# Diagonal and neighbour scores of a recurrence: a sum over partitions by a matrix of ones, in F32R

## The reference, cut to what matters

```python
q = silu(xn @ w_q)
forget = lb + (1 - lb) * sigmoid(xn @ w_f)
log_f, k, v = log(forget), 1 - forget, xn @ w_i
# for each head (8 heads, 128 channels d) and each chunk of time:
b = cumsum(log_f)                                    # over the times of the chunk
o_inter = (q * exp(b)) @ state
scores[t, s] = sum_d q[t, d] * k[s, d] * exp(b[t, d] - b[s, d])   # s <= t, else 0
o = o_inter + scores @ v
state = exp(b_last) * state + (k * exp(b_last - b)).T @ v
```

## Time and profile before

| | us |
|---|---|
| median of 3 runs | 2204.59 (2203.95 to 2204.7) |
| profiled execution, its own time | 2202.08 |
| its span in the profile | 2200.3 |
| PE busy | 2175.3 (99%) |
| DVE busy | 1475.7 (67%) |
| ACT busy | 987.3 (45%) |
| POOL busy | 936.6 (43%) |
| mean granted clock of TensorE | 0.999 |

### The profile page before, as it was taken

One profiled execution on the slowest core, in us unless ns is written; L12 is line 12 of the kernel. 1 busy time (PEld: TensorE's weight loads), 2 busy tenths in 40 slices (PEclk: granted clock), 3 DMA queues, 4 the chain that ended last, 5 costly groups with the idle time before them and its releaser, 6 DMA issues.

```text
span 2200.3 us, 29937 instructions
## 1 busy us (share of the span) xinstructions
PE 2175.3 (99%) x11390; PEld 1828.2 (83%) x11390; DVE 1475.7 (67%) x1967; ACT 987.3 (45%) x1338; POOL 936.6 (43%) x256
## 2 busy tenths in 40 slices
PE   8999999999999999999999999999999999999998
PEld 6888887787798897888887798897788887898887
DVE  6999998777656468877867666467666515656333
ACT  5353564524343344666555343344566524243333
POOL 3444444544553553423224453554411244453542
PEclk9999999999999999999999999999999999999999
DMA  5233332422223333222122223332322222233322
GB/s 199 96 106 106 106 124 74 156 89 86 96 96 102 110 99 103 58 77 58 56 66 88 96 96 96 100 111 80 101 53 62 72 82 91 96 97 101 119 77 77
DMA packets 230851, 206.65 MB, mean 94 GB/s; under 512 B 13905, under 2 KB 220369, under 8 KB 230481
## 3 DMA queue, kind: packets, MB, share of 16 engines
q1 hardware_dynamic: 227328, 199.36, 29.0%
q10 hardware_dynamic: 3408, 5.70, 0.7%
HBM read 194.02 MB, written 4.19 MB: 90 GB/s over the span
## 4 chain that ended last, share of the span: by engine, by line
PE 88%; issue 5%; DVE 3%; POOL 2%; ACT 1%; DMA 0%; POOLq 0%; SPq 0%; ACTq 0%; DVEq 0%
PE ps L2035 15%; PE ps L2037 15%; PE ps L2036 15%; PE ps L2068 5%; PE ps L2069 5%; PE ps L2070 5%; PE ps L2268 5%; PE ps L2266 5%; PE ps L2267 5%; PE ps L2400 2%; POOL w_lo L643 2%; PE ps L2607 2%; PE ps L2568 2%; PE ps L2596 1%; DVE ps L1584 1%
## 5 line engine op out<-in xcount | busy, mean ns | idle before, releaser
L643 POOL TENSOR_TENSOR w_lo<-raw,w_hi 128x2048 fp32r<-128x2048 f32 x149 | 712.9, 4784 | 992.6 <-ACT w_hi L694 982.2
L694 ACT ACTIVATE w_hi<-raw 128x2048 fp32r<-128x2048 f32 x148 | 283.4, 1915 | 523.7 <-PE ps L2037 370.2
L2035 PE MATMUL ps<-XH,w_hi 128*128 128x512 f32 x576 | 228.9, 397 | 0.0
L2037 PE MATMUL ps<-XH,w_lo 128*128 128x512 f32 x576 | 227.5, 395 | 0.0
L2036 PE MATMUL ps<-XL,w_hi 128*128 128x512 f32 x576 | 227.5, 395 | 0.0
L2035 PE MATMUL ps<-FH,w_hi 128*128 128x512 f32 x528 | 208.7, 395 | 0.0
L2036 PE MATMUL ps<-FL,w_hi 128*128 128x512 f32 x528 | 208.6, 395 | 0.0
L2037 PE MATMUL ps<-FH,w_lo 128*128 128x512 f32 x528 | 208.6, 395 | 0.0
L1597 DVE TENSOR_TENSOR ps<-ps,rst 128x1024 f32<-128x1024 f32 (+1 forms) x52 | 55.5, 1067 | 185.7 <-PE ps L2037 136.4
L656 POOL TENSOR_TENSOR w_lo<-raw,w_hi 128x1024 fp32r<-128x1024 f32 x35 | 96.9, 2768 | 175.7 <-ACT w_hi L882 175.7
L1338 DVE SCALAR_TENSOR_TENSOR ps<-UP,vec,ps 128x512 f32<-128x512 f32 x224 | 148.6, 744 | 0.0
(11 more groups left out here) (434 smaller groups left out, 5657.1 us busy)
## 6 DMA issues: line engine op xcount, KB each, us to landing
raw<-in_w SPq DMA_DIRECT2D x64, 512.0 KB, 4.3
raw<-in_mlp_w_up SPq DMA_DIRECT2D x64, 512.0 KB, 4.4
raw<-in_mlp_w_down SPq DMA_DIRECT2D x64, 512.0 KB, 4.3
raw<-in_w_in SPq DMA_DIRECT2D x56, 512.0 KB, 4.6
raw<-in_mla_w_o SPq DMA_DIRECT2D x16, 512.0 KB, 5.0
raw<-in_w_b_out SPq DMA_DIRECT2D x16, 384.0 KB, 3.8
raw<-in_w_a_out SPq DMA_DIRECT2D x8, 512.0 KB, 4.5
raw<-in_w_o SPq DMA_DIRECT2D x8, 512.0 KB, 3.9
```

The costliest lines, as they stand in the source:

```text
L643: pool.tensor_tensor(w_lo[:, s], raw[:, s], w_hi[:, s].bitcast(F32), ALU.subtract)\
L694: act.activation(w_hi[:, s], raw[:, s], ACT.Copy).then_inc(hi_done, 1)
L2035: pe.matmul(dst, his[k], xh[k], start=start and k == 0, stop=False)
L2037: mm = pe.matmul(dst, los[k], xh[k], start=False, stop=stop and k == n - 1)
```

## The change

The diagonal score and the neighbour score no longer come from block products. DVE makes the products over all channels elementwise, HD = HQ * HK (512 columns) and HN = exp * k * q (256 columns, one for each pair). ACT rounds them to F32R (HDH, HNH), DVE makes the rest (HDL, HNL). PE multiplies with ONES, a 128x128 matrix of ones, in two passes (high and low), which puts the sum over the channels into every partition; the masks keep the same places as before. HDL and HNL lie at the addresses of HD and HN. The last level's subtraction, exponential and products run on half as many elements for the decay: one subtraction in place of two, 256 columns of Exp in place of 512, two products of 256 as before, the second waiting for the first. The semaphores used are ones that an earlier stage has left. Where the new steps stand in each engine's order is in the diff:

```diff
@@ ACT
+            act.activation(ONES[:], ones[:], ACT.Copy).then_inc(ff_sem("h_one"), 1)
             act.wait_ge(s_("f_gain"), 2)
...
@@ def decays_act
                 for l in range(len(LEVELS)):
                     act.wait_ge(s_("h_arg"), 14 * h + 2 * l + 2)
-                    act.activation(HE[:, l], HE[:, l], ACT.Exp).then_inc(s_("h_e"), 1)
+                    e = HE[:, l] if l < len(LEVELS) - 1 else HE[:, l].rearrange("p (g u) -> p g u", u=2)[:, :, 1]
+                    act.activation(e, e, ACT.Exp).then_inc(s_("h_e"), 1)
+                act.wait_ge(*ff("h_d", h + 1))
+                act.activation(HDH[:], HD[:], ACT.Copy).then_inc(ff_sem("h_dh"), 1)
+
+            def next_act(h):
+
+                act.wait_ge(s_("h_qk"), 14 * h + 14)
+                act.activation(HNH[:], HN[:], ACT.Copy).then_inc(ff_sem("h_nh"), 1)
@@ def head_act
                     gates_act(h + 1, split=(lambda: split_hi(2 * h + c + 4, 0)) if first else None)
+                if first:
+                    next_act(h)
                 out_gate_act(h, n)
...
                 square_out(h)
+                if more:
+                    next_act(h + 1)
@@ def decays_dve
+                    if m == 1:
+                        dve.tensor_tensor(ev[:, :, 1], bv[:, :, 1], bv[:, :, 0], ALU.subtract).then_inc(s_("h_arg"), 2)
+                        continue
@@ def decayed_dve
+                    if m == 1:
+                        next_ = HN[:].rearrange("p (g t) -> p g t", t=1)
+                        dve.tensor_tensor(next_, ev[:, :, 1], kv[:, :, 0], ALU.mult).then_inc(ff_sem("h_n"), 1)
+                        dve.wait_ge(*ff("h_n", h + 1))
+                        dve.tensor_tensor(next_, next_, qv[:, :, 1], ALU.mult).then_inc(s_("h_qk"), 2)
+                        continue
@@ DVE
+            def same_dve(h):
+
+                dve.wait_ge(s_("hq_done"), h + 1)
+                dve.wait_ge(s_("hk_done"), h + 1)
+                dve.tensor_tensor(HD[:], HQ[:], HK[:], ALU.mult).then_inc(ff_sem("h_d"), 1)
+
+            def same_low_dve(h):
+
+                dve.wait_ge(*ff("h_dh", h + 1))
+                dve.tensor_tensor(HDL[:], HD[:], HDH[:].bitcast(F32), ALU.subtract).then_inc(ff_sem("h_dl"), 1)
+
+            def next_low_dve(h):
+
+                dve.wait_ge(*ff("h_nh", h + 1))
+                dve.tensor_tensor(HNL[:], HN[:], HNH[:].bitcast(F32), ALU.subtract).then_inc(ff_sem("h_nl"), 1)
@@ def head_dve
                 if more and not first:
                     gates_dve(h + 1)
+                if not first:
+                    next_low_dve(h)
                 levels_dve(h, range(2 if first else 0, 4))
                 if more:
                     floor_dve(h + 1)
                 else:
                     keep_dve(0)
+                if first:
+                    next_low_dve(h)
                 levels_dve(h, (4,))
...
                 levels_dve(h, (7,))
                 if more:
+                    same_dve(h + 1)
                     decays_dve(h + 1, range(3, len(LEVELS)))
                     keys_to_end_dve(h + 1, 1 - n)
                     rest_dve(h + 1, 1 - n)
                     decayed_dve(h + 1, 1 - n)
+                    same_low_dve(h + 1)
@@ DVE, head 0
             decays_dve(0, range(len(LEVELS)))
+            same_dve(0)
             keys_to_end_dve(0, 0)
             decayed_dve(0, 0, range(2), last=False)
+            same_low_dve(0)
             rest_dve(0, 0)
@@ def diagonal
                 pe.wait_ge(s_("h_t1"), h + 1)
-                pe.wait_ge(s_("hq_done"), h + 1)
-                for b in range(TB):
-                    t = slice(b * P, (b + 1) * P)
-                    mm = pe.matmul(ps[:, 6, t], HK[:, t], HQ[:, t], start=True, stop=True)
-                mm.then_inc(s_("h_g"), 1)
+                pe.wait_ge(*ff("h_one", 1))
+                pe.wait_ge(*ff("h_dl", h + 1))
+                pe.matmul(ps[:, 6], ONES[:], HDH[:], start=True, stop=False)
+                pe.matmul(ps[:, 6], ONES[:], HDL[:], start=False, stop=True).then_inc(s_("h_g"), 1)
@@ def level
                 pe.wait_ge(s_("h_qk"), 14 * h + 2 * l + 2)
+                if m == 1:
+                    pe.wait_ge(*ff("h_nl", h + 1))
+                    pe.matmul(ps[:, 4 + l % 2, 0:HALF], ONES[:], HNH[:], start=True, stop=False)
+                    pe.matmul(ps[:, 4 + l % 2, 0:HALF], ONES[:], HNL[:], start=False, stop=True)\
+                        .then_inc(s_("h_g"), 1)
+                    return
```

More of the change, by code:

```diff
@@ L189, in build_program @@
             ("FR", [P, T], F32),
+            ("HD", [P, T], F32), ("HDH", [P, T], F32R), ("HN", [P, HALF], F32), ("HNH", [P, HALF], F32R),
+            ("ONES", [P, P], F32R),
         ]
@@ L195, in build_program @@
             at_h += size + (-size) % 32
-        HR, HZ, HQ, HK, HF, HGATE, HVF, HV, HE, HP, HQD, HKD, HEB, reset, HKT, HS, masks, FR = made
+        HR, HZ, HQ, HK, HF, HGATE, HVF, HV, HE, HP, HQD, HKD, HEB, reset, HKT, HS, masks, FR, HD, HDH, HN, HNH, ONES = made
+        HDL, _ = place("HDL", [P, T], F32R, at_h - (4 * T + 4 * T + 4 * HALF + 4 * HALF + 4 * P))
+        HNL, _ = place("HNL", [P, HALF], F32R, at_h - (4 * HALF + 4 * HALF + 4 * P))
         AH, _ = place("AH", [P, HEADS_M, T], F32R, a_xh)
@@ L268, in build_program @@
             "part_kept": ("lru_done", 15), "u_y": ("mu_add", 7), "u_f": ("xc_done", 8), "u_fh": ("uh_done", 8),
-            "u_fl": ("yb_evac", 8), "root_2": ("ch_done", 2), "d_scaled": ("v_part", 36),
+            "u_fl": ("yb_evac", 8), "root_2": ("ch_done", 2), "h_d": ("lam_abs", 2), "h_dh": ("ln_inv", 2), "h_dl": ("pads", 2),
+            "h_n": ("mu_mm", 1), "h_nh": ("var_mm", 1), "h_nl": ("r_row", 1), "h_one": ("lam_e", 1), "d_scaled": ("v_part", 36),
         }
```

## The result

| | before | after |
|---|---|---|
| median, us | 2204.27 (2200.58 to 2204.7, 4 runs) | 2258.14 (2256.74 to 2259.41, 4 runs) |
| profiled execution, its own time | 2202.08 | 2256.74 |
| its span | 2200.3 | 2254.9 |
| mean granted clock | 0.999 | 0.988 |
| PE busy, share of the span | 2175.3 (99%) | 2187.8 (97%) |

The ratio is 1.0248, 95% interval 1.023 to 1.0266: slower by 2.5%. The forecast was 2239 us with a range up to 2254. The sign, the place and the first links of the chain were right. Which instructions stand still, and what the lower clock costs, came out otherwise.

A forecast was written before the change was run, and what follows sets the result against it. PE, busy 99%, was taken to bound the kernel, its gains eaten by new waits. Profiled 2202.08 + 30.2 for waits + 4 for the clock + 2.5 from profiled execution to median = 2239 us, range 2213 to 2254.

The forecast's parts named there:

- E: Mark in each head: the end of DVE's last decayed product, from which the prediction counts its + times.
- The failed step: DVE behind OL: POOL's second instruction takes the lock after X, HNL stands until +14.4, level 2 at about +15.7.
- rival 1: POOL's second instruction starts later or HNL slips in: 0.68 us per head, +10.1 in all, 2215 us; chance 0.15.
- rival 2: POOL takes the lock twice in a row ahead of OL: 1.25 us more per head, 2246 us; chance 0.09.
- The mis-sized term: PE's lower clock after idling in six heads: 4 us taken, bounds 0 and 10.
- L: Mark in each head: PE starts the block of level 2, 11.67 us after E before the change.
- heads 1 to 6, E to L: Late POOL splits and DVE's standing HNL delay level 2: 4.03 us per head, six times, 24.2.
- heads 1 to 6, L to E, clock in it: Behind the last level's copy DVE has 0.37 us more per head; the lower clock adds 4.
- head 0, up to E of head 1: DVE's prologue grows 0.87 us and next_low_dve adds 0.34, +1.2; DVE's later work before E adds 0.37.
- head 7, E to L: No second split, but PE waits for the late chunk: L at E + 12.06 against 9.19, +2.9 us.
- The upper bound: Clock loss between L and the last copy in every one of six heads: 6 x 1.7 = 10 us, sum +40.
- rival 3: PE stays the bound and its 8.0 us come off, 2197 us; chance 0.08 with its partial form.

The follow-up runs named there:

- the wait alone: Kernel before, with only a wait on ACT at the end of each head for the next head's last decayed product: 2252.56 us, ratio 1.0231.
- the filler: Changed kernel with 30 unused F32R matmuls of 256 columns on PE ahead of level 2 in heads 1 to 6: 2243.8 us, ratio 1.0193.
- ACT's move alone: Changed kernel with ACT's HNH copy moved behind the root and the first split of the next head, DVE's order unchanged: 2253.04 us, ratio 1.0235.
- both: Changed kernel with ACT's HNH copy behind the next head's first split and DVE's HNL subtraction behind the state sums: 2215.95 us, ratio 1.0066.

## Why the prediction was wrong

**What held.** ACT's wait for E puts root, splits and POOL late: HNH at +0.03 (forecast +0.13), POOL at +3.58 (+3.67), OL's end at +8.70 (+8.82). L1895, the old victim, is free. PE's chunk is late. PE saves 0.35 at the diagonal and 0.65 at the last level, none of which shows in the time. That the wait alone does nearly all of it was measured.

**The failed step: who has the lock after OL.** The prediction said that POOL's second instruction takes the lock when L1850 (X) leaves it, at +9.48, and that HNL stands. In the trace POOL went on without a break, between OL and X; X stood 5.05 us, and behind it HZ (+13.6, forecast +9.4) and HF came late. HNL, at 0.41 us, was free; the prediction had named that as the sign of rival 1, but here X had taken the stop in its place. The outcome lies between the forecast and rival 2, which had given POOL the lock twice ahead of OL: the two alternate, POOL, OL, POOL, X (an estimate from the ends: with 4.6 us for each of POOL's two, OL and X end some 0.5 us behind one, and the pair's 9.54 us leave 0.34 between them). Level 2 came at +16.55, not +15.7: 0.85 us per head.

**The mis-sized term: the clock.** By E and L of the profiled runs (E of head 1 to E of head 7: 199.8 us before, 244.9 after; the six stretches from E to L sum to 69.51 and 99.56):

| term, us | forecast | measured |
|---|---|---|
| heads 1 to 6, E to L | 24.2 | 99.56 - 69.51 = 30.1 |
| heads 1 to 6, L to E, clock in it | 2.2 + 4 | 45.1 - 30.1 = 15.0 |
| head 0, up to E of head 1 | 1.6 | 932.37 - 930.79 = 1.6 |
| head 7, E to L | 2.9 | 15.13 - 9.19 = 5.9 |
| from there to the last output product, and the rest | -0.65 | 2.1 |
| sum | 34.3 | 54.7 |

From level 2 to level 3 the six steady heads took 30.1 us in place of 17.8, for the same instructions: 12.3 us, which is nearly all that L to E grew by beyond the 2.2 forecast. Taking the idleness away in the filler gave 12.0 back there. The forecast took 4 because one case didn't tell how often, and allowed 10 at most, six times one stretch of 3.4 us at half rate. It happened in every head, since every head has the same idle time, and lasted longer in four of them: 5.33 - 2.96 = 2.37 us lost here, in place of 1.7. Head 7 adds what the forecast had left out: behind its wait of 4.04 us the chunk takes 2.73 us in place of 1.40, levels 1 and 2 stand 4.27 apart in place of 2.3, and level 3 follows after 4.20 in place of 2.96, 4.5 us together. So the term for the clock was 4 and measured some 17. Of the last row but one, 1.2 is this clock; where the other 1.5 us against the forecast come from is open.

The Trainium skill (TensorE: Matmul & The Clock Gate, "HAM oscillation") describes a loop in which every turn idles and every turn then starts at the lower clock. This trace agrees in that (level 2 at a low clock in each of six heads), though PE's work between two idle times is 30 us and more here, where the page's bursts are shorter than its idle times. The upper bound that the prediction tied to that page was nearer than the value taken.

**The range** ended at 2254, which left out both errors together; each alone (+5 for the lock, +13 for the clock) would have stayed inside. Rivals 1 and 3 didn't happen: two instructions of DVE's stood in each steady head, and PE was not what the others waited for.

## What to carry to other kernels

A wait added at the end of a queue is paid by what stands behind it: here a wait placed ahead of ACT's splits moved them 3.1 us later against E (from E - 1.5 to E + 1.6), and by itself it cost 51 us where the whole change cost 54. Put the new step behind everything that is ready, on every engine that has one (by their ratios to before, ACT's move alone gave 0.1%, both gave 1.8%; DVE's move alone was not run), and then read who ends last again, since each repair here uncovered the next wait. When PE sets the pace and is made to idle 4 us in every turn of a loop, price its clock in every turn, not as a chance, and don't take the length of one such stretch for all: here 1.7 to 2.4 us were lost per turn, and 4.5 once.

## What the runs showed of the hardware

- POOL's split and DVE's instructions that read two tensors in SBUF exclude each other, and who gets in next depends on what stands around them. A 512-column instruction of DVE's takes 4.3 to 5.1 us behind POOL in place of 0.7. POOL was held off through a dense run of DVE's (6.04 and 5.82 us in place of 4.6; 8.50 in the earlier trace rows); by an estimate, with the usual 4.6 for its own work, it began in each of the three within 0.15 us of the first instruction in DVE's run that reads PSUM (1034.84, 1037.22 and 899.63).
- A gap of 0.1 to 0.2 us in that run, from a wait of DVE for itself, was enough to let POOL in (4.75 and 4.78 us for a product of 0.42).
- After OL, which had itself stood, POOL's waiting instruction came ahead of X with no gap in DVE's queue that the trace shows, in the steady heads of after, of the wait alone and of the filler. With POOL's second instruction put off (10.5 us behind the first) X is free. Why DVE's run doesn't hold there is open; no run here separates the kind of instruction from the earlier stop.
- After 4.4 us of idleness PE lost 1.7 to 2.4 us to the lower clock in each of the six steady heads (mean clock 0.50 to 0.64 over the 3.4 us from level 2 on); after 3.1 us of it, with ACT's step moved, it was at 0.50 for 5.7 us; after 4.04 us in head 7 it lost 4.5 us. With the idle time filled its mean over the run rose from 0.988 to 0.995 (before: 0.999).
